# Value halves issued one at a time behind earlier weight tiles, and a value projection of 8 tokens in four column tiles

## The reference, cut to what matters

```python
mod = _adaln(c, w_ada, b_ada)                       # 6 x 1024 columns, 12 tiles of 512
h = _normalize(x) * (1 + scale) + shift
qa, ka, va, qb, kb, vb, ga, gb = split(h @ w_in)     # 512 x 3, 768 x 3, 1024 x 2 columns
oa = softmax(qa . [pages of k, own k]) @ [pages of v, own v]     # sample: 2048 past rows each
outs = three dilated windows over kb, vb
mix = (sigmoid(ga) * (oa @ w_proj_a) + sigmoid(gb) * (merge(outs) @ w_proj_b)) @ w_out
x = LN1(alpha * x + gate1 * mix)
x = LN2(alpha * x + gate2 * hierarchical_moe(LN(x)))  # 4 groups of 8 experts, top 2
```

## Time and profile before

| | us |
|---|---|
| median of 3 runs | 1096.56 |
| lowest and highest run | 1094.95, 1098.03 |
| profiled execution | 1094.32 |
| its span in the trace | 1092.2 |
| TensorE, VectorE, ScalarE, GpSimd busy | 847.7, 344.8, 182.7, 115.6 |

### The profile page before, as it was taken

One profiled execution on the slowest core, in us unless ns is written; L12 is line 12 of the kernel. 1 busy time (PEld: TensorE's weight loads), 2 busy tenths in 40 slices (PEclk: granted clock), 3 DMA queues, 4 the chain that ended last, 5 costly groups with the idle time before them and its releaser, 6 DMA issues.

```text
span 1092.2 us, 11668 instructions
## 1 busy us (share of the span) xinstructions
PE 847.7 (78%) x4564; PEld 465.0 (43%) x4564; DVE 344.8 (32%) x520; ACT 182.7 (17%) x429; POOL 115.6 (11%) x116
## 2 busy tenths in 40 slices
PE   6599898989979999992618888777877777877840
PEld 5484676468864454871513323222222222322210
DVE  2048998793243321327411100000000000000018
ACT  2311223222221110003302111101011111111110
POOL 1212211110012112000010000000000000000020
PEclk9799999999998885996658999999999999999975
DMA  9986999587999999999983999999999999999931
GB/s 313 399 316 245 401 408 400 201 323 282 355 359 429 426 393 350 381 365 354 373 328 156 426 425 425 423 426 428 426 426 424 425 427 424 426 427 422 419 113 45
DMA packets 70084, 396.30 MB, mean 363 GB/s; under 512 B 6418, under 2 KB 13094, under 8 KB 47847
## 3 DMA queue, kind: packets, MB, share of 16 engines
q1 hardware_dynamic: 50928, 296.97, 68.2%
q0 software_dynamic: 12016, 85.90, 19.6%
q10 hardware_dynamic: 7104, 12.93, 3.4%
HBM read 387.89 MB, written 58.10 MB: 408 GB/s over the span
## 4 chain that ended last, share of the span: by engine, by line
PE 44%; DMA 37%; DVE 13%; issue 3%; ACT 1%; SPq 1%; ACTq 0%; POOL 0%; POOLq 0%; DVEq 0%
DMA ring<-in_w_exp_up_dram 28%; PE bank L801 12%; PE bank L436 10%; DVE ring L1220 3%; DMA ring<-in_cache_v_pages_dram,pidx 3%; DVE S L1224 3%; PE bank L716 3%; PE bank L446 3%; DMA ring<-in_w_in_dram 2%; PE bank L633 2%; PE bank L703 1%; DMA ring<-in_cache_k_pages_dram,pidx 1%; PE bank L819 1%; PE bank L523 1%; PE bank L462 1%
## 5 line engine op out<-in xcount | busy, mean ns | idle before, releaser
L801 PE MATMUL bank<-ring,hT 128*64 128x512 f32 x1024 | 243.6, 631 | 43.7 <-DMA ring<-in_w_exp_up_dram 41.2
L801 PEld LDWEIGHTS bank<-ring,hT 128*64 128x64 f32 x1024 | 89.7, 144 | 196.2 <-issue 196.2
L1601 DVE TENSOR_TENSOR hT<-hT,bank 128x256 f32<-128x256 f32 x32 | 19.3, 603 | 415.4 <-ACT hT L1144 415.4
L436 PE MATMUL bank<-hT,ring 128*128 128x264 f32 x576 | 140.9, 403 | 5.8 <-DMA ring<-in_w_in_dram 5.8
L819 PE MATMUL bank<-ring,hT 128*64 128x512 f32 x512 | 118.6, 604 | 19.5 <-DVE hT L1604 19.5
L436 PEld LDWEIGHTS bank<-hT,ring 128*128 128x128 f32 x576 | 112.1, 198 | 27.5 <-issue 7.8
L1220 DVE TENSOR_TENSOR ring<-ring,qbc 128x4096 f32<-128x4096 f32 x16 | 70.7, 4417 | 43.1 <-ACTq L846 41.2
L1743 POOL DMA_INDIRECT expert_rows<-work,ridx x32 | 31.1, 971 | 470.4 <-ACT work L838 351.4
L838 ACT ACTIVATE work<-bank 128x512 f32<-128x512 f32 (+5 forms) x83 | 36.6, 451 | 221.9 <-PE bank L819 145.2
L819 PEld LDWEIGHTS bank<-ring,hT 128*64 128x64 f32 x512 | 40.9, 138 | 76.6 <-issue 76.6
L1224 DVE TENSOR_REDUCE S<-ring 128x64 f32<-128x4096 f32 x16 | 70.6, 4414 | 0.3
(11 more groups left out here) (303 smaller groups left out, 783.1 us busy)
## 6 DMA issues: line engine op xcount, KB each, us to landing
ring<-in_w_exp_up_dram SPq DMA_DIRECT2D x32, 2048.0 KB, 22.0
ring<-in_w_exp_down_dram SPq DMA_DIRECT2D x32, 2048.0 KB, 21.8
ring<-in_w_exp_gate_dram SPq DMA_DIRECT2D x32, 2048.0 KB, 17.5
ring<-in_w_ada_dram SPq DMA_DIRECT2D x12, 2048.0 KB, 13.9
out_dram<-in_state_dil_kv_dram SPq DMA_DIRECT2D x6, 4064.0 KB
ring<-in_w_in_dram SPq DMA_DIRECT2D x11, 2048.0 KB, 21.1
out_dram<-in_state_dil_kv_dram ACTq DMA_DIRECT2D x16, 508.0 KB, 7.7
out_dram<-in_state_dil_kv_dram SPq DMA_DIRECT2D x8, 992.0 KB
```

The lines of the kernel that those rows point to most:

```text
L436: i = mm(bk[:, 0:NT], w[:, k, j * P:(j + 1) * P], hT3[:, k, :], start=(k == 0), stop=(k == KC - 1))
L801: i = mm(side(2, half).rearrange("p (m n) -> p m n", m=2), xT[s][:, k, :], w[:, :, k, half * 256:(half + 1) * 256], start=(k == 0), stop=( ...
```

## The change

The sample tokens' third of each value tile is computed by a new function, `win_v8`. It splits the tile's n columns into four parts of n/4, and part j is written to partitions 32j to 32j+7 of one bank, so that the four parts lie in four column tiles of the array: 32 products (64 instructions) of n/4 columns instead of 8 (16) of n. ScalarE copies the four parts with four instructions instead of one.

GpSimd's two waits for the last weight tile ahead of the first two value halves are replaced: the first half waits until ada 10 has landed, the second until win 10 has. All other waits, slots and loads stay.

```diff
+            def win_v8(w, c0, n):
+                bk = take(("v", c0, 2), acc[0] % 2)
+                acc[0] += 1
+                m = n // 4
+                for k in range(KC):
+                    for j in range(4):
+                        i = mm(bk[32 * j:32 * j + NB, 0:m], hT3[:, k, SEQ:NT], w[:, k, j * m:(j + 1) * m],
+                               start=(k == 0), stop=(k == KC - 1))
+                done(("v", c0, 2), i)
+                return i
...
-                        i = win_v(w, *V_TILES[t], tt)
+                        i = win_v(w, *V_TILES[t], tt) if tt < 2 else win_v8(w, *V_TILES[t])
...
-                        i = copy(v[0:tn, tt, c0:c0 + cn], bk[0:tn, 0:cn])
+                        if tt < 2:
+                            i = copy(v[0:tn, tt, c0:c0 + cn], bk[0:tn, 0:cn])
+                        else:
+                            for j in range(4):
+                                m = cn // 4
+                                i = copy(v[0:NB, 2, c0 + j * m:c0 + (j + 1) * m], bk[32 * j:32 * j + NB, 0:m])
...
             for hh in range(2):
                 pool.wait_ge(s_kred, 2 * NB - 1 + hh)
-                if hh == 0:
-                    pool.wait_ge(w_full[slot_of(("win", 11))], ring_use["win", 11][2])
+                last = (("ada", 10), ("win", 10))[hh]
+                pool.wait_ge(w_full[slot_of(last)], ring_use[last][2])
                 page_half(v_pages, 0, hh, VSLOT[hh], v_full[hh])
```

## The result

| | before | after |
|---|---|---|
| median of 15 runs each, us | 1097.21 | 1103.48 |
| ratio, 95% interval | | 1.0061 [1.0047, 1.0075] |
| profiled execution, us (span) | 1094.32 (1092.2) | 1105.84 (1103.8) |

The change costs 6.7 us (5.2 to 8.2); +0.4 was forecast, and 1103.5 lies above the range. The two spans differ by 11.6 us, more than the medians. Up to the issue of the output projection's load, just behind the sample values, the profiles differ by 407.29 - 399.54 = 7.75 us. From there to the end it is 692.7 us before and 696.5 after, and this stretch took 692.7 to 700.5 us in the 18 profiles of this study, whatever was changed ahead of it.

What follows compares the result with a forecast made beforehand. VectorE, TensorE and the DMA engines were taken to limit different stretches. TensorE's run ending 3.2 us later (3.9 - 0.7), less 2.8 in the sample values, made +0.4: 1094.7 profiled, 1097.0 as median; range 1091.0 to 1101.5 us.

Steps and rivals of the forecast that it cites:

- part 1: Sample value projection in column tiles: TensorE's run from 240 to 318 us starts 0.7 us earlier (3.2 earlier to 1.6 later).
- part 2: First two value halves issued earlier: TensorE's run ends 3.9 us later, through a wait and slower clock at win 10.
- Tile 2, cost nothing: Tile 2: the saved 5.07 us only lengthens TensorE's wait on VectorE at 121.16; gain none, clock cost possible.
- Tile 6, 1.5 us earlier: Tile 6: VectorE's 1.40 us wait at 213.16 goes, K pages limit next; 1.5 us taken, ends 0 and 3.24.
- The 0.8 us of clock behind that wait: Products behind TensorE's wait at 239.84: a wait twice as long costs 0 to 1.58 us more; 0.8 taken.
- Win 10, 2.9 + 1.0: Near 291 us: first half delays win 10; TensorE waits 1.8 to 3.9 us (2.9), clock costs 0 to 1.6 (1.0).
- 0.84 MB: Amount of win 10 still to come from 286 us, when the first value half was expected to start moving.
- Win 11, at most 1.2 us and none taken: Two halves ahead land win 11 by 315.4 at the latest, TensorE wants it at 314.2: at most 1.2 us, none taken.
- the slower rival: TensorE pays for the second half too, at win 11 (310.26): 8.3 us in all, 1101.4 to 1102.1 us; chance 0.18.
- Given back, 2.8 us: Sample values, 330 to 400 us: third token's first half lands 9.4 us after issue, not 12.2; 2.8 us less.
- Even sharing: At win 10 the half takes two bytes per weight byte, not seven; TensorE waits 0.4 us; 1091.8 to 1093.5; chance 0.24.
- Column tiles not side by side: Sample tiles: with 8 stationary columns, 64 products take some 7.4 us, no saving; 1097.7 us; chance 0.10.

Runs made afterwards that it cites:

- tile 2 alone: Kernel before with the sample tokens' value projection in column tiles in tile 2 only, value halves as before: ratio 1.0047.
- p2_only: Kernel before with only the waits of the two value halves moved, behind ada 10 and win 10; value projection as before: ratio 1.0031.
- p2_first: Kernel before with only the first value half early, behind ada 10; the second waits for win 11 as before: ratio 1.0051.
- p2_first64: Kernel before with the first value half behind ada 10, loading only 64 of its 128 rows, the second behind win 11: ratio 1.0022.
- a_first_guard: The whole change, but the second value half behind win 11 and the K half near 152 us held until win 5 landed: 1.0027 against the kernel before.
- a_guard: The whole change, plus the K half issued near 152 us held on GpSimd until win 5 has landed: 1.0049 against the kernel before.
- p2_later: Kernel before with the first value half behind win 10 and the second behind adaLN 11: ratio 1.0092.

## Why the prediction was wrong, step by step

Its sum was -0.7 (part 1) + 3.9 (part 2) - 2.8 = +0.4. The profile up to the output projection's load reads +6.5 + 5.0 - 3.75 = +7.75.

- **Tile 2, cost nothing: wrong.** Part 1 came out at +6.5 in place of -0.7, which is 7.2 of the 7.35 us between sum and profile; 6.3 us stood at win 5, as a wait and as slow products behind it. The saving of 5.07 us and the longer waits were right. The text even says that it "can cost: clock", but no cost of it stands in the sum, and the slack was looked for only at TensorE's next wait on VectorE (1.32 us at 151.58). It was lost at another place. A slower stretch releases a ring slot later, SyncE issues the next weight tile later, and that tile had no slack against a K half. Checking the landing of win 5 (156.6) against the first data of the K half issued at 151.86 (154.6) would have shown that the two overlap already, though not what one microsecond more costs. This mechanism is shown for tile 2 alone; in the whole change it is worth 1.3 us of the end (uncertain by more than that), perhaps because what it delays was to be delayed by the halves anyway, which is not shown.
- **Tile 6, 1.5 us earlier: right, at 1.1.** VectorE's wait at 213 is gone. The waits on the last two K pages are 0.57 (none before) and 1.69 (1.84 before): the pages are the next limit, as said. What TensorE is late by falls from 7.76 us in tile 6 (204.83 for 197.07) to 6.62 at its next wait on VectorE (246.46 for 239.84): 1.1 us. The 0.8 us of clock behind that wait did not come: the products took 4.86 us in place of 5.41. In tile 7 the sample tile took 1.08 us.
- **Win 10, 2.9 + 1.0: late as forecast, but too small and by another road.** Six profiles have the first half behind adaLN 10. In five of them (after, p2_only, p2_first, p2_first64, a_first_guard) TensorE waited 3.4 to 3.8 us, in a_guard 2.4, and in all six the products behind took 5.2 to 5.5 us, 1.4 to 1.7 over 3.83. The five give 4.9 to 5.5 together: the upper end of the bounds, not their middle. The failed step is the sharing of what was left of the tile. 0.84 MB was misread: between 286 us and win 10's landing the weight queue moved 255 packets, 0.48 MB, and 96 of the 117 packets of 288 to 292 came after that landing. And the half's first packet moved 4.3 us after its issue, not 3.8 (p2_first, 286.68 for 282.35); from there until its last the weight queue moved 22 packets, 0.05 MB. At the forecast rates so little would have cost no wait. It cost 3.8 us because the last packets lay on what reads as one engine, each behind a page packet. So it is partly luck that the forecast of 2.9 is near.
- **Win 11, at most 1.2 us and none taken: no wait came, but only because TensorE was so late.** In the change win 11 took 22.1 us in place of 13.0, 9.1 more, within the two halves (9.8) of the bound, and landed 1.4 us before its use. Elsewhere the bound does not hold: 24.2 us in a_guard (a wait of 1.42) and 27.8 in p2_later (9.20), where 15 counts were in at 314.47 and the last came at 319.40. The bound left out the state copies, which share the engines, and the last packets of one engine. This is the slower rival's place, and its time (1101.4 to 1102.1) was the nearest of all cases, but in the change its wait did not occur.
- **Given back, 2.8 us: right.** 3.0 in p2_first, 3.75 in the change, whose fifth half landed 8.2 us after its issue (forecast 9.4).
- **The rivals.** Even sharing: no, the wait on win 10 stands in all six profiles. Column tiles not side by side: no, 1.93 us.

By the end of the samples the change costs more than its runs do (7.75 against 6.7, 5.2 to 8.2), which is within what the stretch behind varies. That it all hangs on this end one for one, as the prediction says, can't be told beside such a spread.

## What to carry to other kernels

- Before a load is moved ahead, list each later tile that the DMA engines still have to finish, with its landing and its use. Here a half that moved while win 10's last packets were open put 2.0 to 6.2 us between the last two of its 16 counts (0.5 to 2.0 in the other profiles), though only some 0.05 MB of it was left in p2_first. So ask which engine is through last, not how many bytes are left.
- TensorE time that is saved ahead of a wait need not be free: follow what the wait does to the clock, from there to the slot releases and the loads that hang on them, and look for the transfer with the least slack.
- Where two delays end at the same resource, taking one away shows the other. Take the parts away one after the other before adding up prices.

## What the hardware showed that I had not expected

- 15 of a tile's 16 counts can be in 6 us ahead of the last one. In the change the weight queue moved 7 packets (0.01 MB) in 5 us, 0.77 us apart, while pages moved 116 and state copies 112 (294 to 299 us):

```profile
q0 software_dynamic: 116, 1.90, 88.8%
q10 hardware_dynamic: 112, 0.23, 11.8%
q1 hardware_dynamic: 7, 0.01, 0.6%
```

- A page half of 64 rows took nearly as long as one of 128: its 16 KB packets took 1.13 us each in place of 0.61, at the same busy share (85.1% and 84.8%).
- The same 16 products behind the wait near 121 us took 3.83, 5.5 or 6 us from profile to profile, and one microsecond in the issue that hangs on them decided a transfer race 40 us later.
